# Split fp32 products of a three-layer transformer block: moving operands read backwards, weight slices interleaved by element

## The chip, the cores and the metric

One NeuronCore of one Trainium2 chip runs the whole program in one launch. The metric is the device time of that launch in microseconds (us), median of the runs; nanoseconds are marked ns. TensorE is the matmul engine (PE in the profile, PEld for its weight loads), VectorE is DVE, ScalarE is ACT, GpSimd is POOL, and SyncE (SP) issues the transfers.

## The reference, cut to what matters

The input is 256 tokens of width 1024, float32. Two layers of the first kind follow each other, then one layer of a second kind.

```
for l in range(2):                       # first kind
    h = rms_norm(x) * (1 + scale1) + shift1
    z = h @ w_in[l]                      # 14 column tiles of 128
    mix = concat(attention, short conv, pooling) @ w_out[l]        # 8 tiles
    x = x + gate1 * mix
    h2 = rms_norm(x) * (1 + scale2) + shift2
    # experts: h2 @ peer_wq (16 tiles), top 16 of 128x128 keys per head,
    # then gelu(h2 . expert_u[e]) * gate, weighted sum of expert_v[e]
    x = x + gate2 * peer_ffn(h2, ...)
# second kind: h @ w_in_2 (22 tiles), S5 and SSD mixers, @ w_out_2 (8 tiles),
# cross attention (wq, wk, wv, wo: 8 tiles each),
# conv FFN: h @ w_up (44 tiles), silu(conv(g)) * v, @ w_down (22 tiles)
```

All 16,384 experts of a layer are computed for all tokens, as dense products: 128 units of `expert_u` and 128 units of `expert_v`, each a 128 x 1024 float32 tile of 512 KB; the gate is zero where an expert was not chosen.

## The kernel before, in words

**Units.** Every weight is cut into units of 128 partitions x 1024 floats. `STREAM` lists them in the order of use, and SyncE loads unit `u` into `RING[:, u % 8]` (`SLOTS` = 8) once unit `u - 8` is used up (`stream`). A layer of the first kind has its 14, 8 and 16 units of `w_in`, `w_out` and `peer_wq`, then 256 expert units.

**The split.** A float32 product is made of three fp32r matmuls. ACT rounds the unit to its high part in `RING_HI[:, u % 4]` (`HIGHS` = 4; `split_high`, L352, in the expert loop `high`, L1591), DVE subtracts it and writes the rest into `RING_LO` (`split_low`, L357, in the expert loop `low`, L1680). Activations have a high and a low part too (`H_HI`, `H_LO` and others).

**The products.** `unit_product` (L315 to L317) takes a unit as the stationary operand: for each of the eight slices `k` of 128 weight columns it runs high x high, high x low and low x high, with a moving operand of 128 x 256 (all tokens), into half a PSUM bank. Each of the three matmuls loads its 128 x 128 weights anew. `unit_group` (L494 to L496), the loops at L841 to L843, L2031 to L2033 and L2538 to L2540 do the same with another order of loops, and `unit_spread` (L327 to L329) with one moving operand for all eight slices and eight places in PSUM. `unit_wide` (L340 to L342) is for `expert_v`: the stationary operand is a 128-token half of `E_HI` or `E_LO`, the moving operand 512 columns of the unit, 12 matmuls of 128 x 512 per unit.

**The expert stage.** The first 22 pairs of `expert_u` units (`AHEAD`) are multiplied earlier, while the routing is worked out: L1250 in plain float32 and L1253 to L1255 as split products whose high weights lie in `WK_LO`. The stage itself first runs the `unit_wide` products of 21 such pairs, then steps of four units: two by `first_product` (`unit_product` with `H_HI`, `H_LO`) and two by `second_product` (`unit_wide`). In a step ACT does a gelu, four `high` and one `e_high`, DVE four `low`, `weight` and `rest`, each in that written order; `high` of unit `u` waits for unit `u - 4` to be used up, `low` for `high`, and TensorE for the semaphore `split` of `low`. Behind the last unit the result `Y` is turned from tokens by columns to columns by tokens by 16 transposes (L1575).

**Places in SBUF.** The tensors lie behind each other with small pads (`pad_normed`, 8 floats, `pad_work`, 16 floats, and `Arena.passing`, which sets an offset to 112 floats modulo 128), so that the moving operands `H_HI`, `H_LO`, the high parts and the low parts of the units begin at different offsets within 512 bytes.

Of the kernel before, what the change touches and what calls it, by code (L numbers as in the profile page):

```python
# [30 lines left out]
P = 128  # L31
# [63 lines left out]
PRE = 3  # L95

# [35 lines left out]
I_IN, I_OUT, I_XQ, I_XK, I_XV, I_XO, I_FFN, I_END = (STARTS[DEPTH] + u for u in (V_IN, V_OUT, V_XQ, V_XK, V_XV, V_XO, V_FFN, UNITS2))  # L132

# [19 lines left out]
def program(nc, wstream, consts, mixconst, crow, xT, memT, pos, vec2, s5b, s5c, wglu, wdt, out):  # L153
    ctx = ExitStack()
    with ctx:
# [150 lines left out]

        def parts_of(u):
            return RING_HI[:, u % HIGHS, :], RING_LO[:, u % SLOTS, :]

        def unit_product(pe, dst, u, hi, lo):  # L310

            w_hi, w_lo = parts_of(u)
            for k in range(KD):
                o = slice(k * P, (k + 1) * P)
                pe.matmul(dst, w_hi[:, o], hi[:, k, :], start=(k == 0), stop=False)  # L315
                pe.matmul(dst, w_hi[:, o], lo[:, k, :], start=False, stop=False)  # L316
                mm = pe.matmul(dst, w_lo[:, o], hi[:, k, :], start=False, stop=(k == KD - 1))  # L317
            return mm

        def unit_spread(pe, u, hi, lo, first, last, done=None):  # L320

            w_hi, w_lo = parts_of(u)
            for k in range(KD):
                o = slice(k * P, (k + 1) * P)
                dst = PS[:, 4 + k // 2, (k % 2) * T:(k % 2 + 1) * T]

                pe.matmul(dst, w_hi[:, o], hi, start=(first and k % 2 == 0), stop=False, skip_group_check=True)  # L327
                pe.matmul(dst, w_hi[:, o], lo, start=False, stop=False, skip_group_check=True)  # L328
                mm = pe.matmul(dst, w_lo[:, o], hi, start=False, stop=last, skip_group_check=True)  # L329
# [157 lines left out]
        def unit_group(pe, units, outs, starts):  # L487

            for k in range(KD):
                o = slice(k * P, (k + 1) * P)  # L490
                pe.wait_ge(S("h_low"), k + 1)
                for u, dst, first in zip(units, outs, starts):
                    w_hi, w_lo = parts_of(u)
                    pe.matmul(dst, w_hi[:, o], H_HI[:, k, :], start=(first and k == 0), stop=False, skip_group_check=True)  # L494
                    pe.matmul(dst, w_hi[:, o], H_LO[:, k, :], start=False, stop=False, skip_group_check=True)  # L495
                    mm = pe.matmul(dst, w_lo[:, o], H_HI[:, k, :], start=False, stop=(k == KD - 1),  # L496
                                   skip_group_check=True)
                    if k == KD - 1:
                        mm.then_inc(units_used, 1)
# [128 lines left out]
        for layer in range(DEPTH):  # L628
# [26 lines left out]
            with nc.Block() as block:  # L655
# [31 lines left out]
                def _(pe):  # L687
# [140 lines left out]
                    for k, ready, n in ((6, "pool_low", 1), (7, "pool_low", 2), (0, "mix_low", 1), (1, "mix_low", 2),  # L828
# [3 lines left out]
                        for i in range(PRE):  # L832
# [8 lines left out]
                            pe.matmul(dst, w_hi[:, o], MIX_HI[:, k, :], start=(k == 6), stop=False, skip_group_check=True)  # L841
                            pe.matmul(dst, w_hi[:, o], MIX_LO[:, k, :], start=False, stop=False, skip_group_check=True)
                            mm = pe.matmul(dst, w_lo[:, o], MIX_HI[:, k, :], start=False, stop=(k == 3),  # L843
# [340 lines left out]
            with nc.Block() as block:  # L1184
# [23 lines left out]
                def _(pe):  # L1208
# [25 lines left out]
                    def ahead():  # L1234

                        for p in range(AHEAD):
                            if p >= 2:
                                pe.wait_ge(S("ahead_gelu"), p - 1)
                            for e in range(2):
# [7 lines left out]
                                for k in range(KD):  # L1247
                                    o = slice(k * P, (k + 1) * P)
                                    if u < E0:
                                        mm = pe.matmul(dst, RING[:, u % SLOTS, o], H32[:, k, :],  # L1250
                                                       start=(k == 0), stop=(k == KD - 1))
                                    else:
                                        pe.matmul(dst, WK_LO[:, u % 2, o], H_HI[:, k, :], start=(k == 0), stop=False)  # L1253
                                        pe.matmul(dst, WK_LO[:, u % 2, o], H_LO[:, k, :], start=False, stop=False)
                                        mm = pe.matmul(dst, RING_LO[:, u % SLOTS, o], H_HI[:, k, :],  # L1255
                                                       start=False, stop=(k == KD - 1))
# [229 lines left out]
            with nc.Block() as block:  # L1486
# [45 lines left out]
                def _(pe):  # L1532
# [5 lines left out]
                    def first_product(i, r, bank):  # L1538
                        for e in range(2):
                            made_before(pe, i + e, r)  # L1540
                            unit_product(pe, PS[:, bank, e * T:(e + 1) * T], S_EXP + i + e, H_HI, H_LO)\
# [43 lines left out]
                def _(sc):  # L1585
                    def high(i, r):
# [4 lines left out]
                        sc.activation(RING_HI[:, u % HIGHS, :], RING[:, u % SLOTS, :], ACT.Copy)\  # L1591
# [84 lines left out]
                def _(dve):  # L1676
                    def low(i, r):
                        u = S_EXP + i
                        dve.wait_ge(S("high"), r * SLOTS + (i + 1 - V0 - PRE))
                        dve.tensor_tensor(RING_LO[:, u % SLOTS, :], RING[:, u % SLOTS, :],  # L1680
                                          RING_HI[:, u % HIGHS, :].bitcast(F32), ALU.subtract).then_inc(S("split"), 1)
# [213 lines left out]
        with nc.Block() as block:  # L1895
# [10 lines left out]
            def _(pe):  # L1906
# [116 lines left out]
                def out_group(k):  # L2023
# [4 lines left out]
                    for i in range(PRE):  # L2028
                        w_hi, w_lo = parts_of(I_OUT + i)
                        dst = PS[:, 2 + i, 0:T]  # L2030
                        pe.matmul(dst, w_hi[:, o], MIX_HI2[:, k, :], start=(k == 0), stop=False, skip_group_check=True)  # L2031
                        pe.matmul(dst, w_hi[:, o], MIX_LO[:, k, :], start=False, stop=False, skip_group_check=True)
                        mm = pe.matmul(dst, w_lo[:, o], MIX_HI2[:, k, :], start=False, stop=(k == KD - 1),  # L2033
# [398 lines left out]
        with nc.Block() as block:  # L2432
# [6 lines left out]
            def _(pe):  # L2439
# [92 lines left out]
                for k in range(KD):  # L2532
                    o = slice(k * P, (k + 1) * P)
                    pe.wait_ge(S("o_low"), k + 1)
                    for i in range(PRE):
                        w_hi, w_lo = parts_of(I_XO + i)
                        dst = PS[:, 4 + i, 0:T]
                        pe.matmul(dst, w_hi[:, o], OX_HI[:, k, :], start=(k == 0), stop=False)  # L2538
                        pe.matmul(dst, w_hi[:, o], OX_LO[:, k, :], start=False, stop=False)
                        mm = pe.matmul(dst, w_lo[:, o], OX_HI[:, k, :], start=False, stop=(k == KD - 1))  # L2540
# [388 lines left out]
```

## Time and profile before

| | |
|---|---|
| time, median of 3 runs | 2432.15 us (2429.12 to 2435.14) |
| the profiled execution, its own time | 2441.18 us |
| its span, first to last instruction | 2439.4 us |
| PE busy | 2361.4 us, 97% |
| weight loads busy | 2179.5 us, 89% |
| DVE busy | 1714.9 us, 70% |
| ACT busy | 1130.5 us, 46% |
| POOL busy | 148.5 us, 6% |
| mean granted TensorE clock | 0.984 |

Matmuls overlap in the records: each is shown for 276 ns and more, while the next one starts 113 to 118 ns behind it. What a matmul costs is therefore read from the distance of the starts, in the timeline, and not from its duration.

### The profile page before, as it was taken

What the parts mean: (1) busy time and instruction counts of PE and PEld (TensorE: products, weight loads), DVE (VectorE), ACT (ScalarE), POOL (GpSimd) and SP (SyncE); (2) the same over time, 40 slices, a digit from 0 to 9 for tenths busy, and PEclk for the clock granted to TensorE, in tenths of its full rate; (3) what the DMA queues carried; (4) which work ended last, traced back from release to release, by engine and by line L of the source; (5) the groups of instructions that cost most, each with busy time, mean ns of one, the idle gap of its engine ahead of it and who ended that gap; (6) DMA issues with size and microseconds to landing.
All of it is one profiled execution on the core that took longest, in us unless ns stands there. A gap on an engine that the chain in (4) does not pass through costs nothing. (4 is left out here: it accounts for less than half of the span.)

```text
span 2439.4 us, 39506 instructions
## 1 busy us (share of the span) xinstructions
PE 2361.4 (97%) x15756; PEld 2179.5 (89%) x15756; DVE 1714.9 (70%) x2863; ACT 1130.5 (46%) x1631; POOL 148.5 (6%) x205
## 2 busy tenths in 40 slices
PE   5989999999999999999999999999999999999998
PEld 5879898889999999889899889999999888998998
DVE  7979887676666666678988676556766566655665
ACT  4542355444444444565155444445444423545544
POOL 0000352000000000000055000000000000000000
PEclk8989999999999999999999999999999999999999
DMA  9365445786666666434534686655555523343553
GB/s 357 139 229 167 149 133 168 267 292 241 233 241 232 240 233 223 151 113 150 180 123 137 201 308 207 217 203 189 189 189 189 190 78 104 130 150 134 184 190 104
DMA packets 133556, 460.67 MB, mean 189 GB/s; under 512 B 15152, under 2 KB 16432, under 8 KB 132912
## 3 DMA queue, kind: packets, MB, share of 16 engines
q1 hardware_dynamic: 133424, 458.90, 55.1%
q8 instruction: 84, 1.38, 0.2%
q14 instruction: 48, 0.39, 0.0%
HBM read 445.73 MB, written 13.11 MB: 188 GB/s over the span
## 5 line engine op out<-in xcount | busy, mean ns | idle before, releaser
L1680 DVE TENSOR_TENSOR ring_lo<-ring,ring_hi 128x1024 fp32r<-128x1024 f32 x421 | 507.1, 1223 | 392.6 <-ACT ring_hi L1591 392.6
L315 PE MATMUL banks<-normed_lo,ring_hi 128*128 128x256 f32 x2096 | 593.3, 283 | 1.2 <-DVE ring_lo L357 0.8
L316 PE MATMUL banks<-normed_lo,ring_hi 128*128 128x256 f32 x2096 | 589.1, 281 | 0.0
L317 PE MATMUL banks<-normed_lo,ring_lo 128*128 128x256 f32 x2096 | 589.0, 281 | 0.0
L1591 ACT ACTIVATE ring_hi<-ring 128x1024 fp32r<-128x1024 f32 x421 | 435.9, 1056 | 170.1 <-PE banks L342 156.9
L340 PE MATMUL banks<-ring_hi,work_lo 128*128 128x512 f32 x1024 | 399.4, 390 | 8.2 <-DVE work_lo L1701 4.6
L315 PEld LDWEIGHTS banks<-normed_lo,ring_hi 128*128 128x128 f32 x2096 | 396.8, 189 | 6.7 <-issue 1.3
L317 PEld LDWEIGHTS banks<-normed_lo,ring_lo 128*128 128x128 f32 x2096 | 400.5, 191 | 0.0
L341 PE MATMUL banks<-ring_lo,work_lo 128*128 128x512 f32 x1024 | 399.1, 390 | 0.0
L342 PE MATMUL banks<-ring_hi,work_lo 128*128 128x512 f32 x1024 | 399.0, 390 | 0.0
L316 PEld LDWEIGHTS banks<-normed_lo,ring_hi 128*128 128x128 f32 x2096 | 395.4, 189 | 3.4
L357 DVE TENSOR_TENSOR ring_lo<-ring,ring_hi 128x1024 fp32r<-128x1024 f32 x185 | 225.1, 1222 | 74.4 <-ACT ring_hi L352 73.9
L352 ACT ACTIVATE ring_hi<-ring 128x1024 fp32r<-128x1024 f32 x185 | 194.9, 1055 | 94.3 <-PE banks L317 54.1
L340 PEld LDWEIGHTS banks<-ring_hi,work_lo 128*128 128x128 f32 x1024 | 192.8, 188 | 46.0 <-DVE work_lo L1701 5.4
L342 PEld LDWEIGHTS banks<-ring_hi,work_lo 128*128 128x128 f32 x1024 | 192.8, 188 | 40.2
L341 PEld LDWEIGHTS banks<-ring_lo,work_lo 128*128 128x128 f32 x1024 | 192.4, 188 | 36.4
L1597 ACT ACTIVATE work<-banks 128x512 f32<-128x512 f32 x84 | 50.2, 598 | 370.6 <-PE banks L317 370.6
L1376 POOL TENSOR_TENSOR one_hots<-one_hots,routes 128x512 f32<-128x512 f32 x128 | 136.8, 1069 | 349.6 <-DVE one_hots L1462 343.0
L1462 DVE TENSOR_TENSOR one_hots<-routes,banks 128x1024 f32<-128x1024 f32 x128 | 149.2, 1209 | 11.5 <-ACT routes L1338 9.2
L1278 PE MATMUL banks<-one_hots 128*128 128x128 f32 x1024 | 135.1, 275 | 2.9 <-POOL one_hots L1376 2.7
L1250 PE MATMUL banks<-work,ring 128*128 128x256 f32 x608 | 131.9, 379 | 0.0
L1250 PEld LDWEIGHTS banks<-work,ring 128*128 128x128 f32 x608 | 115.2, 190 | 15.5
(395 smaller groups left out, 3677.5 us busy)
## 6 DMA issues: line engine op xcount, KB each, us to landing
ring<-wstream SPq DMA_DIRECT2D x716, 512.0 KB, 3.3
arena<-wstream SPq DMA_DIRECT2D x96, 512.0 KB, 5.3
spill<-one_hots SPq DMA_DIRECT2D x44, 256.0 KB, 4.2
rstd<-spill SPq DMA_DIRECT2D x16, 256.0 KB, 3.8
pool_and_keys<-spill SPq DMA_DIRECT2D x14, 256.0 KB, 3.9
routes<-spill SPq DMA_DIRECT2D x14, 256.0 KB, 4.8
residual<-xT SPq DMA_DIRECT2D x1, 1024.0 KB, 7.8
arena<-mixconst SPq DMA_DIRECT2D x2, 512.0 KB, 4.4
```

Source lines behind the costliest of these rows:

```text
L315: pe.matmul(dst, w_hi[:, o], hi[:, k, :], start=(k == 0), stop=False)
L316: pe.matmul(dst, w_hi[:, o], lo[:, k, :], start=False, stop=False)
L317: mm = pe.matmul(dst, w_lo[:, o], hi[:, k, :], start=False, stop=(k == KD - 1))
L340: pe.matmul(dst, hi[:, t], w_hi[:, o], start=first, stop=False)
L341: pe.matmul(dst, hi[:, t], w_lo[:, o], start=False, stop=False)
L342: mm = pe.matmul(dst, lo[:, t], w_hi[:, o], start=False, stop=last)
L352: act.mark(act.eng.activation(RING_HI[:, u % HIGHS, :], RING[:, u % SLOTS, :], ACT.Copy), "high")
L357: v.mark(v.eng.tensor_tensor(RING_LO[:, u % SLOTS, :], RING[:, u % SLOTS, :], RING_HI[:, u % HIGHS, :].bitcast(F32), ALU.subtract), "split")
L1250: mm = pe.matmul(dst, RING[:, u % SLOTS, o], H32[:, k, :], start=(k == 0), stop=(k == KD - 1))
L1462: v.mark(dve.tensor_tensor(hots[g % HOTS], J[:, 0:2, 4 * g:4 * g + 4].unsqueeze(3) .to_broadcast([P, 2, 4, P]), IOTA_BANK.unsqueeze(1).uns ...
L1591: sc.activation(RING_HI[:, u % HIGHS, :], RING[:, u % SLOTS, :], ACT.Copy)\
L1680: dve.tensor_tensor(RING_LO[:, u % SLOTS, :], RING[:, u % SLOTS, :], RING_HI[:, u % HIGHS, :].bitcast(F32), ALU.subtract).then_inc(S("spli ...
```

## The change

Three things are done together, in every split product but those of the cross attention's `V` and of the plain float32 products.

1. The moving operand is read from its last column to its first, and the PSUM destination is written from its last column to its first, so that each result lands where it did (`mirrored`, `[:, k, ::-1]`).
2. The high part of a unit that is used as stationary operand is stored with its slices interleaved by element: of `b` slices, element `m` of slice `a b + i` lies at `(a 128 + m) b + i` (`in_turns`). ACT writes it so, DVE reads it so, and a weight load reads 128 elements with a step of `b` elements (`part`). `b` is 2, and 4 in layer 1 (`TURNS`). It is 1 for the `expert_v` units, the first two expert units and the `V` units (`turns`). The low part stays as it was.
3. In `unit_wide` the stationary half of `E_HI` and `E_LO` is every second token instead of 128 tokens in a row; the transposes of `Y` write their results to every second column of PSUM to put that right.

No instruction is added or taken away.

```diff
+TURNS = (2, 4, 2)
...
+def turns(u):
+
+    w = STREAM[u]
+    if w < BASE2:
+        e = w % PER_LAYER - U_EXP
+        return 1 if e >= N_EXP - 2 or (e >= 2 and (e - 2) % 4 >= 2) else TURNS[w // PER_LAYER]
+    return 1 if V_XV <= w - BASE2 < V_XO else TURNS[DEPTH]
...
+        def mirrored(view):
+
+            return view[:, ::-1]
+
+        def in_turns(high, b):
+
+            return high.rearrange("p (a m b) -> p a b m", m=P, b=b)
+
+        def side_by_side(w, b):
+
+            return w.rearrange("p (a b m) -> p a b m", m=P, b=b)
+
+        def part(high, k, b):
+
+            return in_turns(high, b)[:, k // b, k % b]
...
-        def unit_product(pe, dst, u, hi, lo):
+        def unit_product(pe, dst, u, hi, lo, b=None):
...
-                pe.matmul(dst, w_hi[:, o], hi[:, k, :], start=(k == 0), stop=False)
-                pe.matmul(dst, w_hi[:, o], lo[:, k, :], start=False, stop=False)
-                mm = pe.matmul(dst, w_lo[:, o], hi[:, k, :], start=False, stop=(k == KD - 1))
+                pe.matmul(mirrored(dst), part(w_hi, k, b or turns(u)), hi[:, k, ::-1], start=(k == 0), stop=False)
+                pe.matmul(mirrored(dst), part(w_hi, k, b or turns(u)), lo[:, k, ::-1], start=False, stop=False)
+                mm = pe.matmul(mirrored(dst), w_lo[:, o], hi[:, k, ::-1], start=False, stop=(k == KD - 1))
...
-                    t, o, dst = slice(tt * P, (tt + 1) * P), slice(n * 512, (n + 1) * 512), PS[:, 4 + 2 * tt + n, :]
-                    pe.matmul(dst, hi[:, t], w_hi[:, o], start=first, stop=False)
-                    pe.matmul(dst, hi[:, t], w_lo[:, o], start=False, stop=False)
-                    mm = pe.matmul(dst, lo[:, t], w_hi[:, o], start=False, stop=last)
+                    o, dst = slice(n * 512, (n + 1) * 512), PS[:, 4 + 2 * tt + n, :]
+                    pe.matmul(mirrored(dst), part(hi, tt, TT), mirrored(w_hi[:, o]), start=first, stop=False)
+                    pe.matmul(mirrored(dst), part(hi, tt, TT), mirrored(w_lo[:, o]), start=False, stop=False)
+                    mm = pe.matmul(mirrored(dst), part(lo, tt, TT), mirrored(w_hi[:, o]), start=False, stop=last)
...
-            act.mark(act.eng.activation(RING_HI[:, u % HIGHS, :], RING[:, u % SLOTS, :], ACT.Copy), "high")
+            b = turns(u)
+            act.mark(act.eng.activation(in_turns(RING_HI[:, u % HIGHS, :], b), side_by_side(RING[:, u % SLOTS, :], b),
+                                        ACT.Copy), "high")
...
-            v.mark(v.eng.tensor_tensor(RING_LO[:, u % SLOTS, :], RING[:, u % SLOTS, :],
-                                       RING_HI[:, u % HIGHS, :].bitcast(F32), ALU.subtract), "split")
+            b = turns(u)
+            v.mark(v.eng.tensor_tensor(side_by_side(RING_LO[:, u % SLOTS, :], b), side_by_side(RING[:, u % SLOTS, :], b),
+                                       in_turns(RING_HI[:, u % HIGHS, :], b).bitcast(F32), ALU.subtract), "split")
...
-                                        pe.matmul(dst, WK_LO[:, u % 2, o], H_HI[:, k, :], start=(k == 0), stop=False)
+                                        pe.matmul(mirrored(dst), WK_LO[:, u % 2, o], H_HI[:, k, ::-1], start=(k == 0), stop=False)
...
-                            mm = pe.transpose(PS[:, k // 2, (k % 2) * T + tt * P:(k % 2) * T + (tt + 1) * P],
+                            mm = pe.transpose(part(PS[:, k // 2, (k % 2) * T:(k % 2 + 1) * T], tt, TT),
```

`unit_spread`, `unit_group` and the loops at L841, L2031 and L2538 are changed as `unit_product` is, `high` and `low` of the expert loop as `split_high` and `split_low`, L1254 and L1255 as L1253 (mirrored only, since `WK_LO` keeps its order).

## Rows read from the trace of the kernel before

**Rows 1.** The page: busy time of the engines.

```profile
PE 2361.4 (97%) x15756; PEld 2179.5 (89%) x15756; DVE 1714.9 (70%) x2863; ACT 1130.5 (46%) x1631; POOL 148.5 (6%) x205
```

**Rows 2.** Stages: start:end, length, busy (count) per engine, clock, DMA share, GB/s.

```profile
40.00:210.00 170.00, 155.04 (x1167) 147.51 (x1166) 150.24 (x398) 85.39 (x168) 1.16 (x33) 0.92 0.56 199
...
410.00:510.00 100.00, 97.65 (x431) 80.53 (x431) 72.36 (x83) 48.55 (x55) 0.00 (x0) 1.00 0.79 275
510.00:985.00 475.00, 475.00 (x3064) 434.18 (x3063) 306.08 (x352) 219.59 (x256) 0.00 (x0) 1.00 0.68 236
...
1450.00:1935.00 485.00, 485.00 (x3104) 442.23 (x3103) 298.64 (x352) 233.64 (x274) 0.00 (x0) 1.00 0.60 201
...
2255.00:2430.00 175.00, 173.83 (x1479) 173.63 (x1477) 115.09 (x168) 87.58 (x128) 0.00 (x0) 1.00 0.49 163
```

**Rows 3.** Timeline, PE, 1500.05:1509.5: first and last of 33 narrow, 24 wide matmuls.

```profile
1500.11 0.28 PE L315 MATMUL banks<-normed_lo,ring_hi 128*128 128x256 f32 x1
...
1503.88 0.28 PE L317 MATMUL banks<-normed_lo,ring_lo 128*128 128x256 f32 x1
1503.99 0.39 PE L340 MATMUL banks<-ring_hi,work_lo 128*128 128x512 f32 x1
...
1509.21 0.39 PE L342 MATMUL banks<-ring_hi,work_lo 128*128 128x512 f32 x1
```

**Rows 4.** Timeline, PE, 166:170: first and last of 21 matmuls, then a key product.

```profile
166.05 0.28 PE L315 MATMUL banks<-normed_lo,ring_hi 128*128 128x256 f32 x1
...
168.32 0.28 PE L317 MATMUL banks<-normed_lo,ring_lo 128*128 128x256 f32 x1
168.44 1.05 PE L1219 MATMUL banks<-pool_and_keys,arena 128*128 128x128 f32 x8
```

**Rows 5.** Timeline, PE, 225:228: sixteen plain float32 matmuls in a row.

```profile
224.66 3.62 PE L1250 MATMUL banks<-work,ring 128*128 128x256 f32 x16
```

**Rows 6.** Groups, whole span: the changed products and L1250; busy, mean ns, idle before.

```profile
L315 PE MATMUL banks<-normed_lo,ring_hi 128*128 128x256 f32 x2096 | 593.3, 283 | 1.2 <-DVE ring_lo L357 0.8 <-ACT arena L872 0.4
...
L340 PE MATMUL banks<-ring_hi,work_lo 128*128 128x512 f32 x1024 | 399.4, 390 | 8.2 <-DVE work_lo L1701 4.6 <-PEq L1184 3.7
...
L1250 PE MATMUL banks<-work,ring 128*128 128x256 f32 x608 | 131.9, 379 | 0.0
...
L1253 PE MATMUL banks<-normed_lo,work_lo 128*128 128x256 f32 x400 | 122.2, 305 | 0.0
...
L315 PE MATMUL banks<-part_at,ring_hi 128*128 128x256 f32 x224 | 65.3, 291 | 2.6 <-DVE residual L1125 2.4 <-issue 0.2
...
L327 PE MATMUL banks<-part_at,ring_hi 128*128 128x256 f32 x176 | 50.3, 286 | 3.4 <-DVE part_at L2759 3.4
...
L494 PE MATMUL banks<-normed_lo,ring_hi 128*128 128x256 f32 x144 | 41.9, 291 | 0.1
...
L841 PE MATMUL banks<-part_at,ring_hi 128*128 128x256 f32 x48 | 13.9, 289 | 0.0
```

**Rows 7.** Groups, PE, 1450:1935: the narrow matmuls of layer 1's expert stage.

```profile
L315 PE MATMUL banks<-normed_lo,ring_hi 128*128 128x256 f32 x668 | 187.7, 281 | 0.0
```

**Rows 8.** L2539: duration ns min/median/max, first and last start.

```profile
L2539 PE MATMUL banks<-part_at,ring_hi x24: 276/276/280, 2206.8 to 2214.7; 128*128 128x256 f32 x24
```

**Rows 9.** Groups, whole span: the splits and two ACT reads of PSUM.

```profile
L1680 DVE TENSOR_TENSOR ring_lo<-ring,ring_hi 128x1024 fp32r<-128x1024 f32 x421 | 507.1, 1223 | 392.6 <-ACT ring_hi L1591 392.6
...
L1591 ACT ACTIVATE ring_hi<-ring 128x1024 fp32r<-128x1024 f32 x421 | 435.9, 1056 | 170.1 <-PE banks L342 156.9 <-DMA spill<-one_hots 9.7 <-PE banks L317 3.5
...
L1352 ACT ACTIVATE arena<-banks 128x512 f32<-128x512 f32 x128 | 75.8, 596 | 102.4 <-PE banks L1278 101.4
...
L1597 ACT ACTIVATE work<-banks 128x512 f32<-128x512 f32 x84 | 50.2, 598 | 370.6 <-PE banks L317 370.6
```

**Rows 10.** DMA, 410:510: share of the 16 engines in 40 slices, tenths.

```profile
DMA  7570687785858675867868585899998999999999
```

More of the change, by code:

```diff
@@ L325, in unit_spread @@
                 dst = PS[:, 4 + k // 2, (k % 2) * T:(k % 2 + 1) * T]
-                pe.matmul(dst, w_hi[:, o], hi, start=(first and k % 2 == 0), stop=False, skip_group_check=True)
-                pe.matmul(dst, w_hi[:, o], lo, start=False, stop=False, skip_group_check=True)
-                mm = pe.matmul(dst, w_lo[:, o], hi, start=False, stop=last, skip_group_check=True)
+                pe.matmul(mirrored(dst), part(w_hi, k, turns(u)), mirrored(hi), start=(first and k % 2 == 0), stop=False, skip_group_check=True)
+                pe.matmul(mirrored(dst), part(w_hi, k, turns(u)), mirrored(lo), start=False, stop=False, skip_group_check=True)
+                mm = pe.matmul(mirrored(dst), w_lo[:, o], mirrored(hi), start=False, stop=last, skip_group_check=True)
                 if done and k % 2 and k < KD - 1:
@@ L493, in unit_group @@
                     w_hi, w_lo = parts_of(u)
-                    pe.matmul(dst, w_hi[:, o], H_HI[:, k, :], start=(first and k == 0), stop=False, skip_group_check=True)
-                    pe.matmul(dst, w_hi[:, o], H_LO[:, k, :], start=False, stop=False, skip_group_check=True)
-                    mm = pe.matmul(dst, w_lo[:, o], H_HI[:, k, :], start=False, stop=(k == KD - 1),
+                    pe.matmul(mirrored(dst), part(w_hi, k, turns(u)), H_HI[:, k, ::-1], start=(first and k == 0), stop=False, skip_group_check=True)
+                    pe.matmul(mirrored(dst), part(w_hi, k, turns(u)), H_LO[:, k, ::-1], start=False, stop=False, skip_group_check=True)
+                    mm = pe.matmul(mirrored(dst), w_lo[:, o], H_HI[:, k, ::-1], start=False, stop=(k == KD - 1),
                                    skip_group_check=True)
@@ L1540, in first_product @@
                             made_before(pe, i + e, r)
-                            unit_product(pe, PS[:, bank, e * T:(e + 1) * T], S_EXP + i + e, H_HI, H_LO)\
+                            unit_product(pe, PS[:, bank, e * T:(e + 1) * T], S_EXP + i + e, H_HI, H_LO,
+                                         TURNS[layer])\
                                 .then_inc(units_used, 1)
@@ L1590, in high @@
                         sc.wait_ge(units_used, r * SLOTS + (u - HIGHS + 1))
-                        sc.activation(RING_HI[:, u % HIGHS, :], RING[:, u % SLOTS, :], ACT.Copy)\
+                        b = turns(u + SLOTS * (r if isinstance(r, int) else AHEAD))
+                        sc.activation(in_turns(RING_HI[:, u % HIGHS, :], b), side_by_side(RING[:, u % SLOTS, :], b),
+                                      ACT.Copy)\
                             .then_inc(S("high"), 1)
@@ L1679, in low @@
                         dve.wait_ge(S("high"), r * SLOTS + (i + 1 - V0 - PRE))
[L1680 to L1681 removed]
+                        b = turns(u + SLOTS * r)
+                        dve.tensor_tensor(side_by_side(RING_LO[:, u % SLOTS, :], b), side_by_side(RING[:, u % SLOTS, :], b),
+                                          in_turns(RING_HI[:, u % HIGHS, :], b).bitcast(F32), ALU.subtract)\
+                            .then_inc(S("split"), 1)
                     def weight_ahead(p):
@@ L2030, in out_group @@
                         dst = PS[:, 2 + i, 0:T]
-                        pe.matmul(dst, w_hi[:, o], MIX_HI2[:, k, :], start=(k == 0), stop=False, skip_group_check=True)
-                        pe.matmul(dst, w_hi[:, o], MIX_LO[:, k, :], start=False, stop=False, skip_group_check=True)
-                        mm = pe.matmul(dst, w_lo[:, o], MIX_HI2[:, k, :], start=False, stop=(k == KD - 1),
+                        pe.matmul(mirrored(dst), part(w_hi, k, turns(I_OUT + i)), MIX_HI2[:, k, ::-1], start=(k == 0), stop=False, skip_group_check=True)
+                        pe.matmul(mirrored(dst), part(w_hi, k, turns(I_OUT + i)), MIX_LO[:, k, ::-1], start=False, stop=False, skip_group_check=True)
+                        mm = pe.matmul(mirrored(dst), w_lo[:, o], MIX_HI2[:, k, ::-1], start=False, stop=(k == KD - 1),
                                        skip_group_check=True)
@@ L2537, in _ @@
                         dst = PS[:, 4 + i, 0:T]
-                        pe.matmul(dst, w_hi[:, o], OX_HI[:, k, :], start=(k == 0), stop=False)
-                        pe.matmul(dst, w_hi[:, o], OX_LO[:, k, :], start=False, stop=False)
-                        mm = pe.matmul(dst, w_lo[:, o], OX_HI[:, k, :], start=False, stop=(k == KD - 1))
+                        pe.matmul(mirrored(dst), part(w_hi, k, turns(I_XO + i)), OX_HI[:, k, ::-1], start=(k == 0), stop=False)
+                        pe.matmul(mirrored(dst), part(w_hi, k, turns(I_XO + i)), OX_LO[:, k, ::-1], start=False, stop=False)
+                        mm = pe.matmul(mirrored(dst), w_lo[:, o], OX_HI[:, k, ::-1], start=False, stop=(k == KD - 1))
                         if k == KD - 1:
```

10 lines of the change are left out of this document (5 added, 5 removed).

## The prediction

> **What bounds the kernel now.** I read the page's first section first: PE is busy for 97% of the span, DVE for 70%, ACT for 46% [rows 1]. Then the stages: in both expert stages (510 to 985 and 1450 to 1935 us) PE is busy without a gap, in the conv FFN for all but 1.2 of 175 us, while DVE has 35 to 40% to spare there and ACT half [rows 2]. So most of the time is the number of matmuls times the distance of their starts, and only what changes that distance changes the time. That distance isn't in the groups, whose durations overlap; it is in the timeline. At 1500 us 33 narrow matmuls (256 columns) run from 1500.11 to 1503.88: 3.77 / 32 = 117.8 ns each. The 24 wide ones (512 columns) behind them run from 1503.99 to 1509.21: 5.22 / 23 = 227.0 ns [rows 3].
>
> Two more places matter. At 166 us the same line L315 to L317, same shape, runs 21 matmuls from 166.05 to 168.32: 2.27 / 20 = 113.4 ns; and eight key products of 128 columns take 1.05 us with a last duration of 0.275, which makes (1.05 - 0.275) / 7 = 110.7 ns [rows 4]. The plain float32 product L1250 has 16 matmuls in 3.62 us, the last of 0.379 [rows 5, 6], so (3.62 - 0.38) / 15 = 216.0 ns. The expert and FFN stages have a granted clock of 1.00, 2.4 GHz [rows 2]. 216.0 ns are 518 clocks, 6 more than 512 columns would need at one a clock; I take it as the undisturbed pace of a wide matmul. Against it the wide split matmul loses 11.0 ns, 5%. Of a narrow one, 110.7 ns is the shortest distance at which weight loads of 128 columns follow each other here; against it the expert stage loses 7.1 ns, 6%. Something other than shape, waits and clock costs these nanoseconds, and it has at least two settings: the duration shows which one, a median of 276 ns at the faster pace [rows 8] and 281 at the slower [rows 7]. The nearest candidate is that the weight load of the next matmul and the moving operand of this one read SBUF at once.
>
> **The change part by part.** Nothing is added on any queue: no instruction, DMA or wait. SyncE, POOL and the semaphores are untouched; only access patterns differ.
>
> *Which matmuls are touched.* Narrow: 3 x (2096 + 224 + 176 + 144 + 48 + 400) [rows 6], and the two loops of 24 at L2031 and L2539 (the latter in [rows 8]), so 3 x 3136 = 9408. Wide: 3 x 1024 = 3072 [rows 6]. One nanosecond less on each is 12.5 us, 0.5% of the time.
>
> *Mirroring and interleaving, narrow.* The cost of this isn't in the trace, since nothing there is read backwards or with a step. What it should do: if the load reads with twice the step of the moving operand at half the column rate, and both in one direction, the two keep a fixed distance in SBUF instead of sweeping past each other. The high part's loads, two of three, get that step at `b` = 2; the low part's, and all of L1253 to L1255, don't; at `b` = 4 in layer 1 the load runs ahead. So I don't expect the floor for all three. I take 113.4 ns, the pace that this very instruction has where the two streams happen to meet better [rows 4]. How many are at 117.8 now? Layer 1's stage 3 x 668 [rows 7]; layer 0's stage of 475 us and 3064 matmuls solves to about 2020; the FFN's 1479 in 173.8 us are nearly all narrow at 117.5 [rows 2]. That is about 5,480. Of the other 3,930 I take half, since both paces occur there: 7,400 in all. Gain: 7,400 x 4.4 ns = 33 us. The bounds: nothing, or 110.7 ns for all, 7,400 x 7.1 + 2,000 x 2.7 = 58 us.
>
> *Mirroring, wide.* Here all three loads have step 2 and all moving operands are contiguous and backwards, so the mechanism can work fully. But no wide split matmul of the trace shows another pace, so I take the middle between 227.0 and 216.0: 3072 x 5.5 = 17 us. Bounds 0 and 34 us.
>
> *The splits.* ACT writes and DVE reads with a step of 8 bytes, in layer 1 of 16. 1056 ns and 1223 ns now [rows 9]. The nearest row with a step is L1352, which reads PSUM at a step of 128 floats and takes 596 ns for 512 elements; L1597 reads a row in sequence and takes 598 [rows 9]. Lower bound none, upper bound a doubling. Doubled, a step of four units (24 x 117.8 x 2 + 12 x 227.0 x 2 = 11.1 us of PE) would have ACT at 5.1 + 2 x 1.06 and DVE at 7.1 + 2 x 1.22 us, taking the busy shares of 46% and 64% in rows 2. Both fit, and a high part has three units of PE (8 us) between its slot coming free and its use. I cost it at nothing; the cover would be thin only from 40 to 210 us, where DVE is busy for 150.2 of 170 us [rows 2], at most some 5 us a layer.
>
> *The transposes of `Y`* write 32 times 128 columns at a step of 8 bytes; at double their pace some 4 us in all, which I put at nothing as well, inside the range.
>
> *What is late next.* With PE 2 to 3% faster the transfers must follow. In the expert stages the DMA engines are busy for 60 to 68%. From about 460 to 510 us they are at 90% or more already [rows 2, 10]; there and in the same stretch of layer 1 the gain may be lost, 2 x 50 us x 2.4% = 2.4 us. Small, and I leave it in the range.
>
> The Trainium skill speaks against part of this. "SBUF — State Buffer" (section "SBUF: two separate sides") and "Advanced Engine Details and Errata" (section "Memory Cachelines") say that SBUF is read in 16-byte lines and that a reader needs at least two hits on a line for full speed. By that, a step of two floats would be free and `b` = 4 would make every weight of layer 1's high parts slower. No row here reads SBUF with a step, and the sum goes by the rows.
>
> **Sum.** 33 + 17 = 50 us. The profiled execution took 2441.2 us, so 2391; it lies 9.0 us above the median of the runs, which gives 2382 us, 2.1% less.
>
> **The rivals.**
>
> *A, the streams no longer meet at all.* Both floors are reached: 58 + 34 = 92 us, 2340 us. For it: in the wide ones all three loads keep step. Against: a third of the narrow loads doesn't. Chance 0.15.
>
> *B, only part of it works:* the wide ones, or the narrow ones of two layers of three: 10 to 35 us, 2397 to 2422, say 2407. For it: the paces depend on how two streams fall, which the trace shows as settings that hold for whole stages. Chance 0.22.
>
> *C, no change.* The paces come from inside TensorE, and reading order is nothing to it: 2432 us. Against: line, shape and clock are the same at 113.4 and 117.8 ns. Chance 0.11. "TensorE: Matmul & The Clock Gate" (section "Part 2: What happens when you issue a matmul") would give this result: two independent read ports, so that a weight load takes nothing from a running matmul. The two paces of rows 3 and 4 don't refute that, since they don't name their cause.
>
> *D, slower.* The mechanism is the weight load with a step of four floats in layer 1: 84 expert units (668 / 8) and 38 others, 16 loads each, 1952 loads. If such a load takes double, its matmul starts after 2 x 110.7 = 221 ns instead of 117.8, 1952 x 103 = 202 us; with the gains elsewhere about 2590. It decides from 50,000 / 1952 = 26 ns per load upwards. In the milder form, 30 to 60 ns, it is 2390 to 2450. For it: no row excludes it. The two-hits rule of the Trainium skill, quoted above, would lead here. Chance 0.14.
>
> **How the numbers follow.** The forecast itself has 0.38. Forecast, A and B are faster: 0.38 + 0.15 + 0.22 = 0.75. C is within 0.3% (7 us, about what a measurement of this kernel can tell from no change) with 0.11, D slower with 0.14. The range goes from A's 2340 to 2437, just above no change, and leaves out D and the tail of A.
>
> **What would show it.** In the profile after: distances of starts at 600 or 1500 us below 117.8 and 227.0 ns; the median duration of L315 to L317 at 276 or below instead of 281; both expert stages shorter by 10 us or more each, still with PE busy throughout; weight loads of layer 1 as long in the records as those of layer 0; the splits at 1056 and 1223 ns. Equal distances in layers 0 and 1 would say that the step of the load doesn't matter; a layer 1 stage above 485 us would be D. It is wrong if the distances stay, or if idle time appears in PE ahead of L315 or L340 behind a split or a transfer.

## The result, and the profile after

The changed kernel takes 2684.1 us in the median against 2433.6 us in the runs of the kernel before beside it: slower, by a ratio of 1.1025 (95% interval 1.0996 to 1.1054). The forecast was 2382 us. One of its four executions took 3803 us at a granted clock of 0.59; the ratio leaves it out and goes by the other three, whose median is 2683.0 us.

The stages come first, from the profile after, cut where the same work begins and ends. The columns are those of rows 2.

```profile
415.00:515.00 100.00, 99.58 (x427) 83.77 (x426) 72.67 (x83) 47.51 (x54) 0.00 (x0) 1.00 0.78 273
515.00:996.00 481.00, 481.00 (x3058) 442.92 (x3057) 305.12 (x352) 230.73 (x256) 0.00 (x0) 1.00 0.67 233
1078.00:1295.00 217.00, 216.14 (x1121) 206.50 (x1122) 169.26 (x509) 90.20 (x122) 1.12 (x32) 0.98 0.36 114
1534.00:2173.00 639.00, 639.00 (x3095) 601.02 (x3094) 369.41 (x350) 312.69 (x272) 0.00 (x0) 1.00 0.45 151
2494.00:2669.00 175.00, 173.83 (x1478) 173.62 (x1476) 115.47 (x168) 95.69 (x129) 0.00 (x0) 1.00 0.50 163
```

And the mixing stage of layer 1 in the kernel before, which the rows ahead of the prediction don't show:

```profile
1052.00:1217.00 165.00, 163.38 (x1117) 153.76 (x1116) 143.33 (x503) 64.59 (x114) 1.12 (x32) 0.99 0.45 151
```

Layer 0's expert stage takes 481 us instead of 475, the FFN the same 175 [rows 2]. Layer 1, the one with four slices interleaved, takes nearly everything: 639 us for the work that took 485, and 217 for 165. PE is busy throughout and the clock is 1.00 in the expert stages: no wait has come in, TensorE itself goes slower. The timeline shows how. The lines are matmuls (PE) and weight loads (PEld) of a narrow product of layer 1 (L341 to L343 are L315 to L317 of before, L366 to L368 are L340 to L342).

```profile
1699.04 0.40 PE L342 MATMUL banks<-normed_lo,ring_hi 128*128 128x256 f32 x1
1699.15 0.21 PEld L343 LDWEIGHTS banks<-normed_lo,ring_lo 128*128 128x128 f32 x1
1699.28 0.28 PE L343 MATMUL banks<-normed_lo,ring_lo 128*128 128x256 f32 x1
1699.28 0.31 PEld L341 LDWEIGHTS banks<-normed_lo,ring_hi 128*128 128x128 f32 x1
1699.40 0.39 PE L341 MATMUL banks<-normed_lo,ring_hi 128*128 128x256 f32 x1
1699.49 0.33 PEld L342 LDWEIGHTS banks<-normed_lo,ring_hi 128*128 128x128 f32 x1
1699.63 0.40 PE L342 MATMUL banks<-normed_lo,ring_hi 128*128 128x256 f32 x1
...
1700.21 0.40 PE L342 MATMUL banks<-normed_lo,ring_hi 128*128 128x256 f32 x1
```

The loads of the interleaved high part (L341, L342) are 0.31 and 0.33 us long, that of the low part (L343) 0.21. From one L342 to the next it is 0.585 us (1699.04, 1699.63, 1700.21) instead of 3 x 117.8 = 353 ns [rows 3]: 232 ns for two loads, 116 ns each. The matmul whose weights have the step is followed 0.23 us later instead of 0.12. Over the whole stage it is a little less: 639 - 485 = 154 us, of which 1088 wide matmuls take some 6.5 (below), leave 147.5 us for its 1339 stepped loads, 110 ns each.

In layer 0 the narrow matmuls of the same profile are where they were, 48 in 5.53 us, so 5.53 / 47 = 117.7 ns, and the 24 wide ones have gone from 227.0 to 5.36 / 23 = 233.0 ns:

```profile
704.18 0.40 PE L366 MATMUL banks<-ring_hi,work_lo 128*128 128x512 f32 x1
...
709.54 0.40 PE L368 MATMUL banks<-ring_hi,work_lo 128*128 128x512 f32 x1
709.78 0.28 PE L341 MATMUL banks<-normed_lo,ring_hi 128*128 128x256 f32 x1
...
715.31 0.28 PE L343 MATMUL banks<-normed_lo,ring_lo 128*128 128x256 f32 x1
```

The sum of the two: 1952 loads x 116 ns = 226 us, and 3072 wide matmuls x 6.0 ns = 18 us, 244 us; with 110 ns per load it is 215 + 18 = 233 us. The spans differ by 2679.0 - 2439.4 = 239.6 us, between the two. The splits of layer 1's stage on DVE and ACT, about half of which are of interleaved units, have gone from means of 1222 and 1057 ns to 1659 and 1596:

```profile
L1713 DVE TENSOR_TENSOR ring_lo<-ring,ring_hi 128x1024 fp32r<-128x1024 f32 x175 | 286.3, 1659 | 265.5 <-ACT ring_hi L1622 265.1
...
L1622 ACT ACTIVATE ring_hi<-ring 128x1024 fp32r<-128x1024 f32 x175 | 260.5, 1596 | 8.2 <-PE banks L368 5.0 <-PE banks L343 3.2
```

These means mix both kinds of unit. Two single ones, of an interleaved unit each, stand alone in the timeline:

```profile
1701.26 2.13 ACT L1622 ACTIVATE ring_hi<-ring 128x1024 fp32r<-128x1024 f32 x1
1688.60 2.14 DVE L1713 TENSOR_TENSOR ring_lo<-ring,ring_hi 128x1024 fp32r<-128x1024 f32 x1 [7.21 <-ACT ring_hi L1622]
```

So an interleaved unit takes ACT twice its time (2.13 against 1.06 us) and DVE 1.75 times (2.14 against 1.22), and TensorE's load is 1.6 to 1.8 times as long in its record (309 and 330 ns on average against 188 in the kernel before). Whether the slow loads or the slow splits make layer 1 slow is what the first experiments ask.

### The profile page after: what moved, and what is told of

Read it like the earlier page. It is cut to its first block and busy times, and to the rows that moved or that the text cites. A ratio compares the mean times of both kernels' runs of the same rounds, so it can differ in the third digit from the quotient of the medians.

```text
span 2679.0 us, 39506 instructions
## 1 busy us (share of the span) xinstructions
PE 2604.2 (97%) x15756; PEld 2432.1 (91%) x15756; DVE 1817.3 (68%) x2863; ACT 1275.3 (48%) x1631; POOL 148.7 (6%) x205
## 5 line engine op out<-in xcount | busy, mean ns | idle before, releaser
L1713 DVE TENSOR_TENSOR ring_lo<-ring,ring_hi 128x1024 fp32r<-128x1024 f32 x421 | 586.2, 1410 | 487.0 <-ACT ring_hi L1622 485.7
L342 PE MATMUL banks<-normed_lo,ring_hi 128*128 128x256 f32 x2096 | 691.2, 330 | 0.0
L341 PE MATMUL banks<-normed_lo,ring_hi 128*128 128x256 f32 x2096 | 686.1, 327 | 1.0 <-DVE ring_lo L386 0.8
L343 PE MATMUL banks<-normed_lo,ring_lo 128*128 128x256 f32 x2096 | 590.7, 282 | 0.0
L1622 ACT ACTIVATE ring_hi<-ring 128x1024 fp32r<-128x1024 f32 x421 | 530.2, 1317 | 112.4 <-PE banks L368 95.9
L342 PEld LDWEIGHTS banks<-normed_lo,ring_hi 128*128 128x128 f32 x2096 | 524.2, 250 | 1.6
L341 PEld LDWEIGHTS banks<-normed_lo,ring_hi 128*128 128x128 f32 x2096 | 505.7, 241 | 6.0 <-issue 1.3
L366 PE MATMUL banks<-ring_hi,work_lo 128*128 128x512 f32 x1024 | 408.1, 399 | 6.3 <-PEq L1213 3.7
L343 PEld LDWEIGHTS banks<-normed_lo,ring_lo 128*128 128x128 f32 x2096 | 412.2, 197 | 0.0
L367 PE MATMUL banks<-ring_lo,work_lo 128*128 128x512 f32 x1024 | 407.9, 398 | 0.0
L368 PE MATMUL banks<-ring_hi,work_lo 128*128 128x512 f32 x1024 | 407.8, 398 | 0.0
L386 DVE TENSOR_TENSOR ring_lo<-ring,ring_hi 128x1024 fp32r<-128x1024 f32 x185 | 255.0, 1382 | 100.4 <-ACT ring_hi L379 99.2
L379 ACT ACTIVATE ring_hi<-ring 128x1024 fp32r<-128x1024 f32 x185 | 249.1, 1348 | 96.8 <-PE banks L343 52.7
L366 PEld LDWEIGHTS banks<-ring_hi,work_lo 128*128 128x128 f32 x1024 | 202.1, 197 | 41.8 <-issue 4.0
L368 PEld LDWEIGHTS banks<-ring_hi,work_lo 128*128 128x128 f32 x1024 | 202.5, 198 | 37.5
L367 PEld LDWEIGHTS banks<-ring_lo,work_lo 128*128 128x128 f32 x1024 | 202.3, 198 | 34.4
L1279 PEld LDWEIGHTS banks<-work,ring 128*128 128x128 f32 x608 | 115.2, 190 | 15.5
```

Source lines behind the costliest of these rows:

```text
L341: pe.matmul(mirrored(dst), part(w_hi, k, b or turns(u)), hi[:, k, ::-1], start=(k == 0), stop=False)
L342: pe.matmul(mirrored(dst), part(w_hi, k, b or turns(u)), lo[:, k, ::-1], start=False, stop=False)
L343: mm = pe.matmul(mirrored(dst), w_lo[:, o], hi[:, k, ::-1], start=False, stop=(k == KD - 1))
L366: pe.matmul(mirrored(dst), part(hi, tt, TT), mirrored(w_hi[:, o]), start=first, stop=False)
L367: pe.matmul(mirrored(dst), part(hi, tt, TT), mirrored(w_lo[:, o]), start=False, stop=False)
L368: mm = pe.matmul(mirrored(dst), part(lo, tt, TT), mirrored(w_hi[:, o]), start=False, stop=last)
```

## The experiments

Where a run was timed in rounds, its ratio to the kernel before is given with its interval; the others were run once each, and their paces are read from their timelines as above.

**Two slices instead of four in layer 1.**

```diff
-TURNS = (2, 4, 2)
+TURNS = (2, 2, 2)
```

> Interleave of layer 1 set from four slices to two, all else as changed. Theory S (a weight load with a step of four floats takes twice as long): layer 1's narrow matmuls start every 116 to 120 ns as those of layer 0 do in the changed kernel, instead of 230 and 236 ns behind high-part loads; about 1950 loads x 113 ns = 220 us come back, so 2450 to 2470 us, still 20 to 30 us over before because of the wide matmuls (233.3 instead of 226.7 ns, 3072 of them = 20 us). Theory L (layer 1 is slow for another reason: the place of its units in the ring, which differs from layer 0's by six slots, or its splits): little changes, 2600 to 2690 us.

Measured: 2471.9 us, ratio 1.0154 (1.0137 to 1.0171). 212 us are back. Layer 1's expert stage in this run:

```profile
L342 PE MATMUL banks<-normed_lo,ring_hi 128*128 128x256 f32 x670 | 188.9, 282 | 0.0
...
L341 PEld LDWEIGHTS banks<-normed_lo,ring_hi 128*128 128x128 f32 x670 | 130.1, 194 | 1.7
L342 PEld LDWEIGHTS banks<-normed_lo,ring_hi 128*128 128x128 f32 x670 | 129.3, 193 | 1.6
L343 PEld LDWEIGHTS banks<-normed_lo,ring_lo 128*128 128x128 f32 x670 | 126.0, 188 | 0.0
```

A step of two costs a load 5 or 6 ns in its record, and the narrow pace nothing: 48 matmuls in 5.53 us, 117.7 ns. Theory L falls. The time is a little above the expected band, since the wide matmuls are at 5.44 / 23 = 236.5 ns in this run, in layer 0 too, whose code is that of the changed kernel with its 233.0. So the same lines run at two paces in two programs; why is open.

**Only mirrored.** Interleaving taken out, of slices and of token halves.

```diff
-TURNS = (2, 4, 2)
+TURNS = (1, 1, 1)
...
-                    pe.matmul(mirrored(dst), part(hi, tt, TT), mirrored(w_hi[:, o]), start=first, stop=False)
+                    pe.matmul(mirrored(dst), hi[:, tt * P:(tt + 1) * P], mirrored(w_hi[:, o]), start=first, stop=False)
```

> Only the moving operands and destinations mirrored; no slice, no token half interleaved. Theory M (the direction of the moving operand costs or gains by itself): wide matmuls stay near 233 ns and the time near 2455 us, or fall below 226.7 ns and the time below 2434 us. Theory P (only the step of the load costs): wide back at 226 to 227 ns, narrow at 117 to 118 ns on average, time 2434 us within 7.

Measured: 2464.8 us, ratio 1.0136 (1.0119 to 1.0153). Theory P falls. In the expert stages narrow matmuls start every 117.7 ns (5.53 / 47), wide ones every 233.0:

```profile
703.44 0.40 PE L366 MATMUL banks<-ring_hi,work_lo 128*128 128x512 f32 x1
...
708.80 0.40 PE L368 MATMUL banks<-ring_hi,work_lo 128*128 128x512 f32 x1
```

Where the kernel before had its faster narrow pace of 113.4 ns [rows 4], this one has 20 matmuls in 2.24 us, 2.24 / 19 = 117.9 ns:

```profile
165.77 0.28 PE L342 MATMUL banks<-normed_lo,ring_hi 128*128 128x256 f32 x1
...
168.01 0.28 PE L343 MATMUL banks<-normed_lo,ring_lo 128*128 128x256 f32 x1
```

That holds for the whole trace. The faster pace goes with a record of 276 or 277 ns; 1,582 of the 9,408 narrow split matmuls of the kernel before have it, and not one in this run, in the changed kernel or in the run further down that only reads backwards. It is worth some 5 us of the 24 by which this trace is longer than the one of before (2463.7 against 2439.4 us); the wide matmuls make the other 19.

**Only interleaved, by two.** `TURNS` (2, 2, 2), token halves interleaved, everything read and written forwards.

```diff
-            return view[:, ::-1]
+            return view
```

> Interleave of two everywhere and token halves interleaved, moving operands read forwards. If the step of two costs by itself (theory P), wide stay at 233 ns and the time is as with mirroring, 2450 to 2470 us; if the two directions belong together (a load that keeps step with a mirrored stream was to avoid it), this one is worse than mirrored with two: wide 235 ns or more and narrow 120 ns or more, 2480 us or above.

Measured: 2470.5 us, ratio 1.0156 (1.0139 to 1.0173), wide 5.37 / 23 = 233.5 ns, narrow 5.58 / 47 = 118.7. The time is that of mirroring and two together, within the intervals. So mirroring alone costs 1.4%, interleaving by two alone 1.6%, and both together 1.5%: they don't add, and they don't help each other. All three are measured with the places of the tensors as they were; for interleaving no other place was tried.

**Stepped splits, plain loads.** ACT and DVE as in the changed kernel; TensorE loads 128 neighbours.

```diff
-            return in_turns(high, b)[:, k // b, k % b]
+            return high[:, k * P:(k + 1) * P]
```

> ACT and DVE write and read the high part interleaved as in the changed kernel (four in layer 1), but TensorE loads each slice as 128 neighbours, so that the weight columns are permuted among slices (this part of the computation is changed). Theory S: PE's narrow pace in layer 1 falls to 117 to 118 ns although the splits of layer 1 still take some 2100 ns on ACT and 2070 ns on DVE; time 2450 to 2460 us. Theory R (the slow splits hold TensorE up): layer 1 stays slow, above 2600 us.

Measured: 2494.5 us. In layer 1's expert stage the splits are as slow as in the changed kernel, and TensorE doesn't mind:

```profile
L1713 DVE TENSOR_TENSOR ring_lo<-ring,ring_hi 128x1024 fp32r<-128x1024 f32 x178 | 291.5, 1661 | 120.8 <-ACT ring_hi L1622 120.2
L1622 ACT ACTIVATE ring_hi<-ring 128x1024 fp32r<-128x1024 f32 x177 | 261.9, 1584 | 7.6 <-PE banks L368 6.1 <-PE banks L343 1.6
L343 PE MATMUL banks<-normed_lo,ring_lo 128*128 128x256 f32 x672 | 189.5, 282 | 0.0
L341 PE MATMUL banks<-normed_lo,ring_hi 128*128 128x256 f32 x672 | 189.4, 282 | 0.0
```

Theory R falls. The time is 35 us above the expected band. Some 10 us are the wide matmuls, at 5.44 / 23 = 236.5 ns here too instead of 233.3. The other 25 lie between the last wide matmul of layer 0 and the first of layer 1: 386.2 us in this run, 361.6 in the kernel before. Most of that is layer 1's mixing, a stage without cover. In this run:

```profile
1066.00:1248.00 182.00, 166.47 (x1092) 155.14 (x1093) 162.49 (x514) 94.79 (x134) 1.12 (x32) 0.95 0.40 130
```

Against the 165 us of before, 182, with PE idle for 15.5 instead of 1.6 and DVE busy for 162.5, 89%. PE waits there for DVE's splits (L386) five times, 6.7 us together, which it did not before, and the granted clock is 0.95 instead of 0.99. So where the splits are slow and TensorE isn't, DVE comes to hold PE up; how the 17 us divide between the waits and the lower clock behind them was not measured.

**Plain splits, stepped loads.** The reverse.

```diff
-            b = turns(u)
+            b = 1
```

> The reverse of the run before it: ACT and DVE split in plain order at 1060 and 1223 ns, TensorE loads with steps of two and four as in the changed kernel (slices are permuted among columns, this part of the computation is changed). Theory S (the load's step of four costs): layer 1's narrow matmuls still start 230 to 236 ns behind high-part loads, stage of its experts as long as in the changed kernel; the first mixing stage of layer 1 alone gets back some 25 us, since the run before took 25 us there with the slow splits alone; 2650 to 2665 us. Theory R (the splits hold TensorE up): 2450 us.

Measured: 2681.4 us, the whole of the slowdown, with splits at 1222 and 1056 ns:

```profile
L342 PEld LDWEIGHTS banks<-normed_lo,ring_hi 128*128 128x128 f32 x668 | 220.4, 330 | 0.0
L1713 DVE TENSOR_TENSOR ring_lo<-ring,ring_hi 128x1024 fp32r<-128x1024 f32 x175 | 210.5, 1222 | 337.1 <-ACT ring_hi L1622 336.8
L341 PEld LDWEIGHTS banks<-normed_lo,ring_hi 128*128 128x128 f32 x668 | 206.1, 309 | 1.5
```

Theory S holds. Its detail that 25 us would come back ahead of layer 1's experts does not: with TensorE slow, the slow splits are hidden there, and taking them away gives 3 us (425.1 instead of 428.5 us from the last wide matmul of layer 0 to the first of layer 1).

**Eight slices in layer 1.**

```diff
-TURNS = (2, 4, 2)
+TURNS = (2, 8, 2)
```

> Layer 1 interleaved by eight, a step of 32 bytes. If the cost is one access per 16-byte line (theory line), a step of 32 bytes costs the same as one of 16: narrow matmuls 230 to 236 ns behind high-part loads, splits 2100 ns, 2680 to 2700 us. If the cost grows with the step (theory distance), the pace goes to 350 ns or more and the time above 2850 us.

Measured: 2702.0 us in one run, 18 us above four slices, not the 160 and more of theory distance. Layer 1's experts:

```profile
L342 PE MATMUL banks<-normed_lo,ring_hi 128*128 128x256 f32 x668 | 271.0, 406 | 0.0
...
L1622 ACT ACTIVATE ring_hi<-ring 128x1024 fp32r<-128x1024 f32 x175 | 260.8, 1594 | 8.3 <-PE banks L368 5.0 <-PE banks L343 3.3
L342 PEld LDWEIGHTS banks<-normed_lo,ring_hi 128*128 128x128 f32 x668 | 227.0, 340 | 0.0
```

ACT takes the same for steps of 16 and 32 bytes, the load 340 ns for 330. What counts is that no second element lies within 16 bytes, and hardly the distance beyond; theory line holds but for a few nanoseconds per load. A step of 12 bytes was not tried. "SBUF — State Buffer" of the Trainium skill, section "SBUF: two separate sides", says it so: lines of 16 bytes, at least two hits on each for full speed. These runs agree with it at steps of 16 and 32 bytes, for TensorE's load as for ACT and DVE (the group mean of DVE's splits is 1651 ns here and 1659 with four slices).

**Reading backwards, or writing backwards.** From the mirrored-only kernel, `mirrored(dst)` replaced by `dst` in one run, and in the other only the destination mirrored.

```diff
-                pe.matmul(mirrored(dst), part(w_hi, k, b or turns(u)), hi[:, k, ::-1], start=(k == 0), stop=False)
+                pe.matmul(dst, part(w_hi, k, b or turns(u)), hi[:, k, ::-1], start=(k == 0), stop=False)
```

> No interleaving; moving operands read backwards, but PSUM written forwards (the result is mirrored, this part of the computation is changed). If reading SBUF backwards is what costs the wide matmuls 6.3 ns, they stay at 233 ns and narrow at 120/115/118; 2460 us. If writing PSUM backwards does it, the paces are those of the kernel before, 226.7 and 117.5 ns; 2434 us.

> No interleaving; moving operands read forwards, PSUM written backwards (the result is mirrored, this part of the computation is changed). The other half of the run before: 226.7 and 117.5 ns, 2434 us, if the direction of the reading costs; 233 ns and 2460 us, if the direction of the writing does.

Measured: 2464.5 us reading backwards, 2438.1 us writing backwards, with 2434.8 for the kernel before on the same chip. The wide matmuls, first of the run that reads, then of the one that writes backwards:

```profile
705.50 0.40 PE L366 MATMUL banks<-ring_hi,work_lo 128*128 128x512 f32 x1
...
710.87 0.40 PE L368 MATMUL banks<-ring_hi,work_lo 128*128 128x512 f32 x1
```

```profile
709.99 0.39 PE L366 MATMUL banks<-ring_hi,work_lo 128*128 128x512 f32 x1
...
715.20 0.39 PE L368 MATMUL banks<-ring_hi,work_lo 128*128 128x512 f32 x1
```

5.37 / 23 = 233.5 ns against 5.21 / 23 = 226.5. So it is the direction of reading in SBUF that costs; the direction of writing in PSUM costs the wide matmuls nothing. The narrow ones of the conv FFN are even faster in the run that writes backwards. First the kernel before, then that run:

```profile
2299.74 0.28 PE L317 MATMUL banks<-normed_lo,ring_lo 128*128 128x256 f32 x1
...
2301.86 0.28 PE L317 MATMUL banks<-normed_lo,ring_lo 128*128 128x256 f32 x1
```

```profile
2299.81 0.28 PE L343 MATMUL banks<-normed_lo,ring_lo 128*128 128x256 f32 x1
...
2302.53 0.28 PE L343 MATMUL banks<-normed_lo,ring_lo 128*128 128x256 f32 x1
```

19 matmuls make 2.12 / 18 = 117.8 ns before, 25 make 2.72 / 24 = 113.3 ns here. This is the pace that the prediction hoped for, in some 1,480 matmuls (by 4.4 ns each an estimated 6.5 us), and it came with the writing direction, not with the reading one. It is one execution, and its whole time is no shorter than that of the kernel before beside it; whether it would come again was not looked for.

**Other places, nothing mirrored.** The kernel before, with the pad ahead of the working tensor and the high parts (16 floats) set to 48, 24 and 8.

```diff
-        sb("pad_work", [P, 16])
+        sb("pad_work", [P, 48])
```

> The kernel before with 128 bytes more between the normed tensors and the high parts (pad_work 48 floats instead of 16), forwards, no interleaving. Theory A (what the load of the next weights costs the moving operand depends on where both lie within 512 bytes): the paces of narrow matmuls whose next load is a high part, 117.5 and 118.3 ns, and of the wide ones, 226.7 ns, shift by 2 ns or more, up or down; by up to 50 us in all. Theory N (addresses don't matter): every pace within 0.5 ns and 2434 us within 7.

> As the run before with 32 bytes more instead of 128 (pad_work 24 floats). Theory A: another shift than with 48 floats. Theory N: 2434 us within 7.

> As the two runs before with 32 bytes less (pad_work 8 floats). Theory A: another shift again. Theory N: 2434 us within 7.

Measured: 2458.2, 2474.4 and 2464.2 us, against 2430.4 us for the kernel before on the same chip. Theory N falls: with nothing but a pad changed, 28 to 44 us go. The first and last of 24 wide and of 48 narrow matmuls with 24 floats:

```profile
705.44 0.40 PE L340 MATMUL banks<-ring_hi,work_lo 128*128 128x512 f32 x1
...
710.81 0.39 PE L342 MATMUL banks<-ring_hi,work_lo 128*128 128x512 f32 x1
711.04 0.28 PE L315 MATMUL banks<-normed_lo,ring_hi 128*128 128x256 f32 x1
...
716.63 0.28 PE L317 MATMUL banks<-normed_lo,ring_lo 128*128 128x256 f32 x1
```

| pad, floats | wide, ns | narrow, ns |
|---|---|---|
| 16 (before) | 227.0 | 117.8 |
| 48 | 5.32 / 23 = 231.3 | 5.59 / 47 = 118.9 |
| 24 | 5.37 / 23 = 233.5 | 5.59 / 47 = 118.9 |
| 8 | 5.31 / 23 = 230.9 | 5.58 / 47 = 118.7 |

The plain float32 matmuls of the ahead products don't move with the pad, although their operands `ring` (ahead of the pad) and `work` (behind it) do change place against each other. With 24 floats:

```profile
L1250 PE MATMUL banks<-work,ring 128*128 128x256 f32 x608 | 131.9, 379 | 0.0
```

The group is as in rows 6, and 15 of these matmuls take 3.40 us in that run's timeline at 224.78, so (3.40 - 0.38) / 14 = 215.7 ns.

**Mirrored, with another place.** The mirrored-only kernel with 48 floats.

> Only mirrored (no interleaving) and pad_work 48 floats. If the 6.6 ns that mirroring costs the wide matmuls are a matter of the places (theory A), they change by 2 ns or more against 233.3 ns here, and mirroring may come out even or ahead; if reading backwards costs by itself (theory B), they stay at 233.3 ns and the time near 2465 us.

Measured: 2463.6 us, wide 5.37 / 23 = 233.5 ns, narrow 5.54 / 47 = 117.9. Theory B by its numbers: the pad that costs 4 ns forwards moves nothing backwards. One pad is little, though, and that no place would make mirroring come out even is not shown. None of the twelve experiments beats the kernel before, which stands at 2430 to 2435 us beside them; the one that writes backwards (2438.1 us, one run) can't be told from it.

## Why the prediction was wrong

**What bounds the kernel** was read rightly. All of the change is in the distance of the starts, no wait came in, and the DMA share fell with the pace. The counts held: with 1952 loads and 3072 wide matmuls the span's difference comes out to within 7 us.

**The step that failed** is the narrow one, "at `b` = 4 in layer 1 the load runs ahead", taken with a gain of 4.4 ns. A load whose elements lie 16 bytes apart takes 309 to 330 ns instead of 188 and puts the next matmul off by 110 to 116 ns. The prediction gave this step no cost at all but counted these loads into its gain; the run without it (two slices) has 212 us back, and the run with plain splits and stepped loads has the whole slowdown. That was rival D, put at 103 ns per load, 202 us and about 2590 us. The mechanism and the count were right there. Its size was a little low (103 ns instead of 110 to 116, 202 us instead of 215 to 226), and its "gains elsewhere" of 50 us were losses, which makes the rest of the way from 2590 to 2684. It had a chance of only 0.14, though no row of the trace spoke against it and the two-hits rule of the Trainium skill, as the prediction quotes it, leads to a slow load at just this step. For the splits the prediction had a row with a step, L1352, but that row reads PSUM; its 596 ns say nothing of a step in SBUF, where the same engine, ACT, took twice its time. The range, which left D out, fell with that.

**Mirroring, narrow:** forecast 33 us of gain; measured none in the expert stages, 117.7 ns against 117.8, and a loss where the kernel before ran at 113.4 ns, 117.9 in the mirrored one. The 113.4 ns of rows 4 are a real pace of the instruction, but reading backwards takes it away instead of bringing it about, some 5 us in all.

**Mirroring, wide:** forecast 17 us of gain, bounds 0 and 34. The sign is wrong: 233.0 instead of 227.0 ns, 18 us of loss. The bound at nothing was set by taking the best case of a mechanism for the only one; no row excluded a loss. Its floor of 216.0 ns came from L1250, a plain float32 product of 256 columns, and was taken over to split matmuls of 512; no run shows one of those below 226.5 ns.

**The mechanism behind both,** that the load of the next weights and the running matmul get in each other's way in SBUF, is not shown. The pads show a part of it: places alone move the wide pace by 4 to 6.5 ns. That it is the distance between the two operands they don't show. The wide matmuls of L340 have both operands, `ring_hi` and `E_HI` in `work_lo`, behind the pad, so that their distance stays the same, and the matmul behind them still starts later with each other pad (229.9 to 235.9 ns on average over an expert stage, 227.2 and 228.2 in the two stages of before); that may come from the matmul of L341 beside it, whose `ring_lo` lies ahead of the pad. Nor does it follow that a fixed distance is better than sweeping past, and the runs show no gain from one: forwards and backwards, with a step of two and without, the kernel before has the best wide pace of all that was tried except for the run that reads as it does. "TensorE: Matmul & The Clock Gate" of the Trainium skill, section "Part 2: What happens when you issue a matmul", has two read ports on which a load takes nothing from a running matmul. That gave rival C here. The pads speak against C as it was put, that the paces come from inside TensorE: they are 227.0 to 233.5 ns for the same instructions, by the place of the operands. Against the two ports themselves no run speaks, since none shows what the place acts on.

**The splits** were bounded well. Twice the time on ACT and 1.75 times on DVE is what they took in layer 1, by the bound of a doubling, and in the expert stage the cover held: with plain loads TensorE keeps its pace beside them. In the mixing stage it doesn't hold, which the prediction named for 40 to 210 us and put at 5 us a layer; in layer 1 it is 17 us in the mixing (182 against 165) and 25 us up to the experts, when the loads are plain. In the changed kernel even this is hidden, by a slower TensorE.

**The transposes and the transfers** can't be told apart from nothing in the sums.

## What to carry to other kernels

Keep the step of an SBUF operand below 16 bytes, for weight loads, ACT and DVE alike: at 16 bytes they took 1.6 to 2 times as long. A step of 8 bytes is far cheaper but not always free: the load's record grows by 5 to 9 ns, ACT's split from 1056 ns to as much as 1227, DVE's not at all, and the kernel with steps of two alone is 1.6% slower. A slow weight load shows neither as idle time nor as a wait: look at the LDWEIGHTS records and at the distance of the matmul starts. Where TensorE is the bound, moving the operands by 32 to 128 bytes was worth 1 to 2%, and a sweep over a pad costs one run per value; a model of why one place is better is not to be trusted without it. A change of access pattern that costs 1 to 2% is of the same size, so a pad should be swept with it before it is judged.

## What the runs showed that was not expected

- Reading the moving operand backwards costs a wide matmul 6 to 7 ns, and a narrow one nothing at 117.8 ns, but its faster pace of 113.4 ns is gone; writing PSUM backwards costs neither anything (226.5 ns wide), and in its one run the conv FFN had the pace of 113.3 ns.
- A matmul starts 0.11 to 0.14 us behind the start of its load even when the load is 0.33 us long; it is the next matmul that comes late (0.23 us).
- Layer 0's wide matmuls run at 233.0 ns in the changed kernel and at 236.5 with two slices throughout, though the code of that layer is the same. What sets this was not looked for.
- A pad of 32 bytes more costs the kernel 44 us in one run, and the plain float32 products nothing.
